# One moving operand for retention's values and gates: two weight units of 256 columns read as one of 512

## What is computed

```python
def token_mixer(u, w_in, ...):
    p = split_columns(u @ w_in)
    branches = (gla_mixer(...), swa_mixer(...), moba_mixer(...),
                retention_mixer(p['ret_q'], p['ret_k'], p['ret_v'], p['ret_g'], ret_norm_g))
    ...                                  # merged = sum_i sigmoid(gate_i) * (o_i @ w_branch[i])
    return merged @ w_out

def retention_mixer(q, k, v, g, norm_g):
    ...                                  # q, k rotated; v: 4 heads of 64 columns
    kv = jnp.einsum('bhnjd,bhnje->bhnde', kc * key_decay[...], vc)
    ...
    o = rms_norm(o, norm_g) * jax.nn.silu(g.astype(f32).reshape(B, S, H, DV))
    return o.reshape(B, S, H * DV).astype(q.dtype)

for l in range(DEPTH):
    h = h + token_mixer(rms_norm(h, ln1_g[l]), w_in[l], ...)
    h = h + hier_moe(rms_norm(h, ln2_g[l]), ...)
return rms_norm(h, final_g)
```

## Time and profile before

| | |
|---|---|
| median of 3 runs | 1430.91 us |
| the profiled execution | 1429.91 us |
| its span, between first and last instruction | 1428.1 us |
| PE busy | 1364.5 us (96%) |
| VectorE, ScalarE, GpSimd busy | 436.6, 438.1, 485.0 us |
| mean DMA rate over the span | 232 GB/s |
| granted TensorE clock over the span | 0.989 of full speed |

### The profile page before, as it was taken

How to read it: one execution, slowest core, us unless ns; L and a number is a source line. 1 busy time by engine, 2 the same in 40 slices (tenths; PEclk the granted TensorE clock), 3 DMA queues, 4 the chain that set the end, 5 groups by cost and what they waited for, 6 DMA issues and landing times.

```text
span 1428.1 us, 19194 instructions
## 1 busy us (share of the span) xinstructions
PE 1364.5 (96%) x7730; PEld 958.5 (67%) x7730; DVE 436.6 (31%) x980; ACT 438.1 (31%) x787; POOL 485.0 (34%) x240
## 2 busy tenths in 40 slices
PE   7999999999999999988999999999999999998986
PEld 6889877888888633333388888778888884333333
DVE  3232754101333421211333437531003243211114
ACT  4522476222332211111254326742223311111112
POOL 2643333555750111111144342336566401111101
PEclk9999999999999999999999999999999999999999
DMA  7522222233377899999973212123343789999997
GB/s 260 194 90 89 75 75 75 74 111 135 109 254 298 345 413 419 420 420 415 410 265 104 89 61 86 62 75 111 96 147 136 257 322 389 421 419 420 420 414 304
DMA packets 136466, 331.24 MB, mean 232 GB/s; under 512 B 16629, under 2 KB 98629, under 8 KB 113848
## 3 DMA queue, kind: packets, MB, share of 16 engines
q1 hardware_dynamic: 127736, 314.29, 58.6%
q0 software_dynamic: 8640, 15.69, 2.9%
HBM read 312.17 MB, written 33.55 MB: 242 GB/s over the span
## 4 chain that ended last, share of the span: by engine, by line
PE 77%; DMA 14%; DVE 3%; SPq 2%; ACT 2%; issue 1%; POOL 0%; DVEq 0%; POOLq 0%; ACTq 0%
PE ps L589 18%; PE ps L591 17%; PE ps L590 17%; PE ps L1010 13%; DMA w<-in_w 12%; SPq L482 2%; PE ps L802 1%; PE ps L809 1%; DMA yb<-y_dram 1%; PE ps L788 1%; PE ps L1002 1%; PE ps L908 1%; PE ps L957 1%; DMA raw<-in_w_in 1%; PE ps L1022 1%
## 5 line engine op out<-in xcount | busy, mean ns | idle before, releaser
L589 PE MATMUL ps<-uH,ringH 128*128 128x512 f32 x704 | 275.6, 392 | 0.0
L591 PE MATMUL ps<-uH,ringL 128*128 128x512 f32 x704 | 274.3, 390 | 0.0
L590 PE MATMUL ps<-uL,ringH 128*128 128x512 f32 x704 | 274.2, 390 | 0.0
L1010 PE MATMUL ps<-w,xT 128*64 128x512 f32 x1024 | 228.4, 597 | 14.0 <-DMA w<-in_w 13.2
L1010 PEld LDWEIGHTS ps<-w,xT 128*64 128x64 f32 x1024 | 77.4, 138 | 157.8 <-issue 151.2
L1449 POOL TENSOR_TENSOR ringL<-raw,ringH 128x2048 fp32r<-128x2048 f32 x28 | 128.7, 4604 | 80.6 <-ACT ringH L1159 80.6
L591 PEld LDWEIGHTS ps<-uH,ringL 128*128 128x128 f32 x704 | 132.2, 188 | 27.8
L589 PEld LDWEIGHTS ps<-uH,ringH 128*128 128x128 f32 x704 | 132.2, 188 | 27.5
L590 PEld LDWEIGHTS ps<-uL,ringH 128*128 128x128 f32 x704 | 132.2, 188 | 27.0
L1010 PE MATMUL ps<-w,hT 128*64 128x512 f32 x512 | 124.1, 629 | 26.1 <-DMA w<-in_w 14.3
L1493 POOL TENSOR_TENSOR ringL<-raw,ringH 128x2048 fp32r<-128x2048 f32 x32 | 147.2, 4599 | 4.8 <-ACT ringH L1307 4.8
(11 more groups left out here) (285 smaller groups left out, 1991.6 us busy)
## 6 DMA issues: line engine op xcount, KB each, us to landing
w<-in_w SPq DMA_DIRECT2D x176, 1024.0 KB, 17.8
raw<-in_w_in SPq DMA_DIRECT2D x54, 1024.0 KB, 5.2
w<-in_w SPq DMA_DIRECT2D x32, 512.0 KB, 18.6
raw<-in_w_out SPq DMA_DIRECT2D x8, 1024.0 KB, 5.1
yb<-y_dram SPq DMA_DIRECT2D x8, 1024.0 KB, 16.1
braw<-in_w_branch SPq DMA_DIRECT2D x24, 256.0 KB, 4.4
h_dram<-hs SPq DMA_DIRECT2D x2, 2048.0 KB, 11.6
y_dram<-attT SPq DMA_DIRECT2D x8, 512.0 KB, 8.9
```

The lines of the kernel that those rows point to most:

```text
L589: mm(o, h, rh, start=first, stop=False)
L590: mm(o, h, rl_, start=False, stop=False)
L591: return mm(o, l, rh, start=False, stop=last)
L1010: ins = mm(o[r], lhs[:, r], rhs[x], start=first, stop=last, skip_group_check=True)
```

## The change

The two units are multiplied in one pass. Halves 13 to 16 become a new kind D, one per token tile: the tile of `uH` or `uL` stands still, and the moving operand is 512 columns, 256 out of slot 0 (`rg`) and 256 out of slot 3 (`rv`). Each half has 24 matmuls of 512 columns, and its bank then holds the gates in columns 0 to 255 and the values in columns 256 to 511. ScalarE reads a bank with two activations: silu into `sr`, then the copy into `vv`, and only the second frees the bank. Each D half waits until the low part of unit 8 is there. The ring slot of unit 7 counts as used after half 16 in place of 14 (`used_at`), so the load of unit 11 is issued later. `chunk_kv(1)`, which reads the values of all tiles, goes from behind half 16 to behind half 17, and its waits for the banks are adapted.

```diff
-          ("T", 5, 128, "sv"), ("T", 6, 0, "rq"), ("T", 6, 128, "rk"), ("R", 7, 0, "rv"), ("R", 7, 1, "rv"),
-          ("R", 8, 0, "rg"), ("R", 8, 1, "rg"), ("T", 9, 0, "mq"), ("T", 9, 128, "mq"), ("T", 10, 0, "mk"),
+          ("T", 5, 128, "sv"), ("T", 6, 0, "rq"), ("T", 6, 128, "rk"), ("D", 7, 0, "rvg"), ("D", 7, 1, "rvg"),
+          ("D", 8, 2, "rvg"), ("D", 8, 3, "rvg"), ("T", 9, 0, "mq"), ("T", 9, 128, "mq"), ("T", 10, 0, "mk"),
...
     if u < U_GATE:
-        return max(2 * u + 1, 2)
+        return max(2 * u + (3 if u == 7 else 1), 2)
...
                 if u or lay:
-                    pe.wait_ge(unit_low.h, unit_low.at(lay, u + 1))
+                    pe.wait_ge(unit_low.h, unit_low.at(lay, (u if kind != "D" else 8) + 1))
...
+                elif kind == "D":
+                    for k in range(KD):
+                        rh, rl_ = (w[:, 0:RING:RING - 1, k * 256:(k + 1) * 256] for w in (ringH, ringL))
+                        last = mm3(bank(b).rearrange("p (a n) -> p a n", a=2), uH[:, k, tmc(off)], uL[:, k, tmc(off)], rh, rl_,
+                                   k == 0, k == KD - 1)
...
                 if br:
-                    pe.wait_ge(bank_freed[0].h, bank_freed[0].at(lay, 8))
+                    pe.wait_ge(bank_freed[0].h, bank_freed[0].at(lay, 9))
+                    pe.wait_ge(bank_freed[1].h, bank_freed[1].at(lay, 8))
...
-                      11: window_values, 12: lambda: out_transposes(0), 13: rotate, 15: lambda: scores(1), 16: lambda: chunk_kv(1),
+                      11: window_values, 12: lambda: out_transposes(0), 13: rotate, 15: lambda: scores(1), 17: lambda: chunk_kv(1),
...
-                elif name in ("gv", "rv"):
+                elif name == "rvg":
+                    bank_full(q)
+                    fn(sr[:, off, :], bank(q % 2, 256), ACT.Silu)
+                    fn(vv[:, off, :], bank(q % 2)[:, 256:512], ACT.Copy).then_inc(bank_freed[q % 2].h, 1)
+                elif name == "gv":
                     copy_out(q, vv[:, 2 * off:2 * off + 2, :].rearrange("p t n -> p (t n)"))
-                elif name in ("gr", "rg"):
+                elif name == "gr":
                     copy_out(q, sr[:, 2 * off:2 * off + 2, :].rearrange("p t n -> p (t n)"), ACT.Silu)
```

## The result

| | before | after |
|---|---|---|
| median of 20 runs each | 1430.23 us | 1432.88 us |
| lowest and highest | 1429.15, 1431.68 | 1430.89, 1436.44 |
| the profiled execution | 1429.91 us | 1431.77 us |
| PE busy, matmuls | 1364.5 us, 7730 | 1362.9 us, 7538 |

What follows compares the result with a forecast made beforehand. The prediction took PE, 77% of the chain of waits, as the bound; 1.2 us saved per layer, 2.4 over both, gave 1427.5 us from the profiled execution or 1428.5 from the median, range 1426.6 to 1430.8.

Steps and rivals of the forecast that it cites:

- TensorE's terms: Halves 13 to 16: 512-column matmuls replace pairs of 256, saving 1.2 us per layer, 2.4 over both.
- ScalarE: Reading each retention half with two activations frees its bank about 0.8 us after filling; wanted 5.5 us later, so no cost.
- unit 8: Half 13 now also needs the gates' weights; their low part is ready 2.6 us before it starts, so no wait.
- the late load: Unit 11's load is issued at about 125.3, ScalarE's split done at 132.5; margins about 7 and 5 us.
- The step that failed: At the changed projection stage, time saved on PE moves the kernel's end unless another engine becomes last to arrive.
- The one on the slower side: Unit 11's late load delays ScalarE's head squares and PE's transposes; slowest landing costs 8.5 us a layer, 1445.5; chance 0.05.
- Only the columns count: In the changed halves, 512 columns over two slots pay the fixed 13 ns twice; time stays 1430.9; chance 0.05.
- the Trainium skill's rule of a fixed gap of 2.5 ns: For the changed halves, two matmuls of 256 columns against one of 512 differ by 2.5 ns; whole change saves 0.5 us.
- The signs named: Prediction wrong if the new spacing exceeds 0.233, PE waits for unit 8, or the span moves while the halves don't.

Runs made afterwards that it cites:

- 191 waits: The kernel after with 191 long-satisfied semaphore waits per layer added to PE's program ahead of the experts: 1428.73 us, ratio 0.9982 to the kernel before.
- 100 waits: The kernel after with 100 long-satisfied semaphore waits per layer added to PE's program ahead of the experts: 1428.48 us, ratio 0.9989 to the kernel before.
- 32 waits: The kernel after with 32 long-satisfied semaphore waits per layer added to PE's program ahead of the experts: 1430.82 us, ratio 1.0004 to the kernel before.
- 16 waits: The kernel after with 16 long-satisfied semaphore waits per layer added to PE's program ahead of the experts: 1438.07 us, ratio 1.0062 to the kernel before.

## Why the prediction was wrong

- **TensorE's terms** held: 0.26 for half 13 (0.29 measured), 0.64 for 14 and 15 (0.58), 0.28 for 16 (0.35): 1.2 a layer, 2.4 in all. With the jumps at their places of before (191 waits) the time fell by 2.2 us, interval 1.3 to 3.9, and with the jumps at other places without a stall (100 waits) by 1.4. The forecast lies in both intervals.
- **ScalarE, unit 8, the late load**: no cost, as forecast. No wait of PE ahead of half 13 or behind half 20; the split of unit 11 at 130.0 where 131 was named.
- **The step that failed** is the sentence that time saved on PE there moves the end, as long as no other engine becomes the last to arrive. It treats PE as its instructions' times alone. That the change takes 191 instructions out of PE's program in each layer was never priced; it moved the jump at the end of the experts to the start of a block. That cost 4.96 us in the first layer and 0.2 in the second, 5.1 or so in all. 5.1 - 2.4 = 2.7 against the 2.65 measured. That it fits so closely is partly luck, for the costs are from one profile and a stall's size differs between runs. Between the changed stage and the sum, the kernel after gained 1.4 us more than the saving in the first layer (3.35 ahead less 0.72 less 1.2) and lost 1.4 in the second (1.80 behind at the sum against 0.40 at the transposes of retention's output). That lies within what runs of one kernel differ by (1429.15 to 1431.68).
- **The rivals**: none named this. The one on the slower side had another mechanism (the load of unit 11), and 0.06 for all slower outcomes was too little for a kernel whose PE program has a branch. "Only the columns count" is out by the spacing of 0.227. By the Trainium skill's rule of a fixed gap of 2.5 ns the stage would have saved a fifth of what it did. But that section ("TensorE: Matmul & The Clock Gate", "Back-to-back issue gap") gives this formula for a single matmul by itself, so it was not a rule on exactly this. It says itself that a stream of pairs of weight load and matmul, as here, is paced otherwise.
- **The signs named** for a wrong prediction (spacing, unit 8, the span moving while the halves don't) did not fit the case: the halves moved and the span moved the other way. A better sign would have been a new wait on "issue" behind a jump in PE's list. That overlapping durations are summed in PE's busy time was wrong too: it is their union.

The best version is the change with the jumps kept off the start of a block: 1428.73 with 191 waits and 1428.48 with 100, both below the kernel before in their own comparisons.

## What to carry to other kernels

- A program with a branch has places that depend on how many instructions stand ahead of it. Where an edit adds or removes instructions on the engine that bounds the kernel, count them, and see where its jumps come to lie in blocks of 256; a loss that shows as waits on "issue" behind a jump is repaired with harmless instructions ahead of it.
- Before an edit is judged by a time difference of 0.2 to 0.4%, run it and the kernel before at the same places of the jumps: here the same edit read 0.19% slower and 0.18% faster.

## What the runs showed of the hardware

- A jump over some 245 instructions cost PE 3.0 to 4.6 us of standstill when it lay less than 20 instructions into its 16 KB block, 2.2 us at 32 and 46, and nothing at 100 to 207; at 238 it was 0.56 us, where PE soon ran into the block behind the target's. At 12 and 16 the target is in the very next block. The Trainium skill ("Runtime: NRT & Kernel Launch", section "Instruction fetch mechanics") names a stall only for a target outside of the current window of two blocks; here the measured 3.4 to 4.6 us differ from it, and they decide. The DMA share was 0.97 to 1.03 in the two stretches shown; no run had the engines idle there, so how much of it is contention stays open.
- The stalls of 3.0 to 4.6 us cost more than themselves, for the granted clock behind each was 0.50 to 0.59; behind the stalls of 2.2 us it fell to 0.53 in one (32 waits, first layer) and stayed at 1.00 in the two others. With 16 waits, at the end of the second layer, 4.2 us without work are followed by 5.4 us at 0.50 of full speed (the same columns as above):

```profile
1411.80:1416.00 4.20, 0.08 (x2) 0.00 (x0) 0.69 (x1) 0.60 (x1) 2.15 (x1) 0.83 0.97 400
1416.00:1421.40 5.40, 5.29 (x13) 4.15 (x14) 1.94 (x3) 0.78 (x1) 0.18 (x1) 0.50 0.16 65
```

- The 512-column form over two slots 24 KB apart goes at 0.227 us a matmul, as that over neighbouring slots.
